# Late groups of a fused expert layer: a slot's twelve products of the whole token tile first, then its eight of the remaining 64 tokens

## The reference

```
q = xb @ w_q                        # 8 heads, two halves of 128
sv, si = top_k(scores against 2 x 128 sub-keys, 16)
eidx = the 16 best pairs of each head, of 16384 experts
gw = softmax(their scores)
u = exp_u[eidx];  v = exp_v[eidx]
a = gelu(einsum('td,thkd->thk', xb, u))
out = einsum('thk,thkd->td', gw * a, v)
```

## Time and profile before

| | |
|---|---|
| median of 3 runs | 1869.37 us (1867.86 to 1870.65) |
| the profiled execution's own time | 1869.01 us |
| its span, first to last instruction | 1867.3 us |
| TensorE (PE) products busy | 1828.4 us, 98% |
| TensorE weight loads (PEld) busy | 1597.0 us, 86% |
| VectorE busy | 1474.4 us, 79% |
| ScalarE busy | 838.0 us, 45% |
| chain that ended last | PE 88%, DVE 8% |

### The profile page before, as it was taken

One profiled execution on the slowest core, in us unless ns is written; L12 is line 12 of the kernel. 1 busy time (PEld: TensorE's weight loads), 2 busy tenths in 40 slices (PEclk: granted clock), 3 DMA queues, 4 the chain that ended last, 5 costly groups with the idle time before them and its releaser, 6 DMA issues.

```text
span 1867.3 us, 25968 instructions
## 1 busy us (share of the span) xinstructions
PE 1828.4 (98%) x10425; PEld 1597.0 (86%) x10425; DVE 1474.4 (79%) x1968; ACT 838.0 (45%) x1138; POOL 393.1 (21%) x257
## 2 busy tenths in 40 slices
PE   7999999999999998999999999999999999999997
PEld 6888888888788998999777889889889899898895
DVE  6544655566773797985888999999899999999996
ACT  5443456344442101224555555455455455455552
POOL 1000223000000011111333323323333333334220
PEclk9999999999999999999999999999999999999999
DMA  8645342856354877988999999999999999999992
GB/s 349 241 180 180 135 136 99 329 181 228 110 203 158 248 286 282 415 327 282 369 367 382 369 395 382 393 381 403 387 381 405 382 386 401 383 385 400 369 359 78
DMA packets 102696, 566.08 MB, mean 303 GB/s; under 512 B 9536, under 2 KB 34176, under 8 KB 36272
## 3 DMA queue, kind: packets, MB, share of 16 engines
q1 hardware_dynamic: 52848, 374.37, 52.6%
q0 software_dynamic: 23168, 164.88, 21.9%
q10 hardware_dynamic: 26560, 25.17, 4.1%
HBM read 547.52 MB, written 14.68 MB: 301 GB/s over the span
## 4 chain that ended last, share of the span: by engine, by line
PE 88%; DVE 8%; DMA 2%; issue 1%; ACT 1%; POOL 0%; SPq 0%; DVEq 0%; ACTq 0%; POOLq 0%
PE bank L1034 14%; PE bank L630 11%; PE bank L647 9%; PE bank L967 6%; PE bank L970 6%; PE bank L1036 6%; PE bank L966 6%; PE bank L969 6%; PE bank L968 6%; PE bank L632 6%; PE bank L932 4%; PE bank L952 2%; DMA spread_b<-bpair 1%; PE bank L870 1%; DVE rows L1822 1%
## 5 line engine op out<-in xcount | busy, mean ns | idle before, releaser
L630 PE MATMUL bank<-act_split,ring_hi 128*128 128x512 f32 x896 | 320.4, 401 | 10.6 <-DVE ring_lo L1455 10.3
L1444 DVE TENSOR_TENSOR ring_lo<-ring_raw,ring_hi 128x2048 fp32r<-128x2048 f32 x90 | 205.8, 2290 | 133.3 <-ACT ring_hi L1097 132.9
L1947 DVE TENSOR_TENSOR split_a<-experts,split_a 128x2048 fp32r<-128x2048 f32 x120 | 274.6, 2288 | 42.9 <-ACT split_a L1370 41.2
L1370 ACT CAST split_a<-experts 128x2048 fp32r<-128x2048 f32 x120 | 229.6, 1913 | 138.6 <-PE bank L970 138.0
L1034 PE MATMUL bank<-h_split,split_a 128*128 128x352 f32 x944 | 260.5, 354 | 0.1
L632 PE MATMUL bank<-act_split,ring_lo 128*128 128x256 f32 x896 | 251.5, 281 | 0.0
L604 POOL DMA_INDIRECT rows<-in_peer_u,eidx x64 | 158.2, 2472 | 381.8 <-DVE rows L1822 381.2
L1036 PE MATMUL bank<-h_split,split_a 128*128 128x176 f32 x944 | 230.7, 244 | 0.0
L604 POOL DMA_INDIRECT rows<-in_peer_v,eidx x64 | 154.8, 2419 | 301.7 <-DVE hrow L1828 280.7
L630 PEld LDWEIGHTS bank<-act_split,ring_hi 128*128 128x128 f32 x896 | 169.1, 189 | 52.4 <-DVE act_split L1455 9.4
L1097 ACT CAST ring_hi<-ring_raw 128x2048 fp32r<-128x2048 f32 x90 | 171.8, 1909 | 87.2 <-PE bank L647 72.0
(11 more groups left out here) (297 smaller groups left out, 3442.1 us busy)
## 6 DMA issues: line engine op xcount, KB each, us to landing
experts<-in_stream SPq DMA_DIRECT2D x221, 1024.0 KB, 9.0
ring_raw<-in_stream SPq DMA_DIRECT2D x91, 1024.0 KB, 4.9
late_raw<-in_stream SPq DMA_DIRECT2D x35, 1024.0 KB
gate_matrix<-stage ACTq DMA_DIRECT2D x12, 1024.0 KB, 11.0
gbuf<-gate_matrix ACTq DMA_DIRECT2D x16, 768.0 KB, 15.6
w<-in_w SPq DMA_DIRECT2D x4, 1024.0 KB, 8.9
gb<-in_ln_g POOLq DMA_DIRECT2D x3, 1024.0 KB, 5.8
gb<-in_ln_b POOLq DMA_DIRECT2D x3, 1024.0 KB, 9.5
```

The costliest lines, as they stand in the source:

```text
L630: pe.matmul(bank[n % 2][:, :], hi[:, k * P:(k + 1) * P], act_split[:, k].rearrange("p c t -> p (c t)"), start=(k == 0), stop=False, skip_g ...
L1370: act.copy(split(m)[0], tile).then_inc(split_hi, 1)
L1444: dve.tensor_tensor(ring_lo[:, r, :], ring_raw[:, r, :], ring_hi[:, r, :].bitcast(F32), ALU.subtract).then_inc(lo_ready, 1)
L1947: dve.tensor_tensor(lo, raw_slot(split_slot(m))[0], hi.bitcast(F32), ALU.subtract).then_inc(split_lo, 1)
```

## The change

In the late groups the loop over a slot's four chunks, which made five products a chunk and went back and forth between the two accumulators, becomes two loops: first the three `whole` products of all four chunks, then the two `rest` products of all four. The products are the same, and each accumulator gets its own in the same order. `whole_products` and `rest_products` were there for the last group's j = 3. The wait for `w_ready` stays ahead of each chunk's `whole` products. `split_used` is raised by the last `rest` product. The early groups (which also use `split_products`) and the last group's j = 3 are untouched.

```
                             if j == 0:
                                 pe.wait_ge(w_ready, 8 * g + c + 1)
                             cols = slice(c4 * 512, (c4 + 1) * 512)
-                            last = split_products(c, hi[:, cols], lo[:, cols], bank[2 + j % 2], j, c == 0, c == 7)
+                            whole_products(c, hi[:, cols], lo[:, cols], bank[2 + j % 2], c == 0, c == 7)
+                        for c4 in range(4):
+                            cols = slice(c4 * 512, (c4 + 1) * 512)
+                            last = rest_products(4 * half + c4, hi[:, cols], lo[:, cols], j)
                         last.then_inc(split_used, 1)
```

## The result

| | before | after |
|---|---|---|
| median of 20 runs each | 1868.05 us (1863.54 to 1870.65) | 1872.10 us (1868.00 to 1875.52) |
| profiled execution's own time | 1869.01 us | 1870.14 us |
| its span | 1867.3 us | 1868.4 us |
| late part: first late second-kind slot to the first fold | 739.69 us | 744.17 us |

The change makes the kernel slower by 0.2%: ratio 1.0020, 95% interval 1.0012 to 1.0027. That is 3.7 us by the ratio and 4.1 by the medians.

What follows compares the result with a forecast made beforehand. The prediction took TensorE, always busy in the late groups, as the bound: number of products times their spacing. Order 0 plus waits 5.1 us, added to the median of 1869.37, gave 1874.5 us, range 1871.0 to 1877.5.

Steps and rivals of the forecast that it cites:

- Part 1: Late second-kind slots on TensorE: fewer accumulator changes gain 0.0 us, bounds 1.2 us more to 10 us less.
- Part 2: Second slot of eleven late groups: TensorE waits for chunk 6's weights, 5.1 us in all, bounds 4.2 to 6.7.
- The restart: TensorE resuming after each wait for chunk 6: signal plus load to product, 0.13 to 0.16 us a group.
- my two values: Time from TensorE's weight load to its product after a wait: 0.11 or 0.08 us, read from the earlier trace.
- Chunk 7 follows for nothing: Second slot: chunk 7's weights, there at 0.79 us, precede its first product at 0.82, so no added cost.
- B: Second slot of late groups: the wait does not come or is taken up; 1869.4 us, chance 0.09.
- D: Late groups: wait costs more than its length, by clock (1909 us) or restart and `split_b` (1877.3); chance 0.06 together.
- C: Late second-kind slots: a run into one accumulator is cheaper, 10 us less; 1864.5 us with the waits, chance 0.05.
- rival A: Late groups: eleven short waits, spacing unchanged; 1874.5 us, own range 1873.6 to 1876.1, chance 0.74.

Runs made afterwards that it cites:

- e5: Kernel before, old order, but all five products of a chunk add into one accumulator in late second-kind slots; 1868.04 us in one run, late part 739.69.
- e6: e4 with accumulators exchanged product by product, some 15 changes a slot, new operand order kept; 1865.60 us in one run, late part 738.67.
- e1: Changed kernel, but each late group's second second-kind slot (j = 0, half = 1) keeps the old order; ratio to before 0.9994, median 1865.52 us.
- e2: Kernel before, old order, but at j = 0, half = 1 the wait for chunk 6's weights moved ahead of the seventh product; ratio 1.0035, median 1873.94 us.
- e4: Changed kernel with VectorE's gathered row of i = 7 moved behind the weights of chunks 6 and 7; ratio to before 0.9995, median 1866.84 us.
- e3: Changed kernel with its two loops exchanged, `rest` products ahead of `whole` products; ratio to before 1.0072, median 1881.86 us.

## Why the prediction was right, point by point

**Part 1, the order.** I took 0 for all slots, within +1.2 and -10 us. Measured is -1.0 (739.69 - 738.67). So the term is mis-sized by 1.0, within its bounds. On `split_a` the working nearly holds: 4.658 us a slot against 4.662 before, where the sum had 4.666 for both; over its slots this is 0.2 us. On `split_b`, where I had no row of a pure sequence and bounds of +1.2 and -2.6, it is 0.8 us. Its slots, forecast at 4.62 to 4.67 us with the others, took 4.58. e5 and e6 show that the premise, that changes of accumulator are free, is right, and that what the order gains has another cause.

**Part 2, the wait.** Its place (chunk 6, second slot), its releaser (`w_low`) and its count (eleven) came as forecast, and e1, e2 and e4 show that it is the cause. The size: 744.17 - 738.67 = 5.50 us against the 5.1 I took from a span of 5.0 to 5.4. Read from the changed trace, chunk 6 is ready 0.28 to 0.39 us later than the seventh product could have started, 3.7 us in all (3.6 forecast). The restart is 0.05 for the signal and 0.11 from load to product, eleven times 0.16, 1.8 us. With 0.16 a group the forecast was 5.4, so most of the miss is in the restart.

That the 0.11 stood among my two values is partly luck. In the earlier trace rows neither product was held back by its load. The one at 1031.23 came the usual 0.23 behind the product ahead,

```profile
1031.00 0.40 PE L970 MATMUL bank<-split_a,w_split 128*64 128x512 f32 x1
```

so the wait there cost nothing, and its 0.11 is no more than an upper bound of the restart. The 0.08 was that of a load in a running stream. Only the changed kernel and e3 show the restart itself, by the 0.34 us to the next product instead of 0.23.

**Chunk 7 follows for nothing.** So it did, by little: in group 7 its load waited for the signal and started 0.09 us later than it could, and the product started in time all the same, in all eleven groups. The margin worked out was 0.03 us. e3, which has two products between the first of chunk 6 and the first of chunk 7 where the changed kernel has three, brings the second wait.

**Nothing takes up the wait, and the clock stays.** 4.48 = 5.50 - 1.02 in the late part, and the granted clock of 1.00 there rule out rivals B and D. What C needs, a cheaper run into one accumulator, is excluded by e5. Its price did turn up: the `whole` products on `split_b` run at 0.227 us in the new order, like the 0.2267 of `row_slot`, but only there, and also when they change accumulator (e6). On the average over all slots the gain is 0.6 ns a product.

**The sum.** Forecast 5.1 us more and 1874.5; measured 4.05 (medians of the larger number of runs, whose kernel before stands at 1868.05 and not at 1869.37) and 1872.1. The difference of 2.4 is 1.3 us in the base, 1.0 in the order, and the other way 0.4 in the waits. The 0.4 left lies between the late part (4.48) and the medians (4.05), well within the interval of the ratio, 2.2 to 5.0 us. 1872.1 is below the own range of rival A, which began at 1873.6, and inside the full range only because that was widened downward; had the base been 1868.05 in the forecast, A's range would have begun at 1872.3. (The prediction's 1872.1 for A with the scatter should read 1873.6 - 1.3 = 1872.3.) The rise came out right at the edge of what I had called measurable.

## What to carry to other kernels

Before you reorder work on the engine that is never idle, write down for each operand when it is ready and when the new order first wants it. An order that has the same instructions and saves next to nothing can still use up the margin of one operand: here 0.65 us in hand became 0.3 us too late, eleven times. And work that hides behind another engine has a size: one gathered row of 2.28 us, behind or ahead of the weights on VectorE, decided between 0.2% slower and no change.

When the whole time scatters by some us, compare the untouched part and the changed part of two profiles separately. Here spans differ by 1.1 us, and the part with the change by 4.48.

## What the runs showed of the hardware that I had not expected

- The late part repeats to 0.01 us between executions of different kernels (739.69 twice, 738.67 twice, 738.66), while the part ahead of it, with the same code in six of them, starts the late groups anywhere within 4.7 us. All of that arises ahead of the early groups' first second-kind slot, which starts between 865.29 and 869.98 us: from there to the late part the eight kernels with the old order in the early groups took 221.11 to 221.15 us. Where ahead of it the time goes wasn't followed.
- The same product, 128 x 512 with `fp32r` operands, costs 0.2331 us from `split_a` in the old order and 0.2329 in the new, and from `split_b` 0.2303 and 0.2287 (slot means over 20), whatever bank it adds to. The spread is between 0.227, for `whole` products in a row on `split_b`, and 0.233. Only the place of the operands and what precedes them differ. The cause stays open; no run tests it.
- A product that had to wait for its weights starts 0.11 us behind the load's start, read from the 0.34 us to the next product. In e3 both products that waited in a group, 0.65 us apart, show these 0.34 us, so a second wait close behind the first pays it again.
